# Order of the tokens in a one-layer streaming encoder: five tiles in one pass, or three dense tiles first and tile 3 with the samples after them

## The chip, the cores and the metric

The kernel runs on one core of one Trainium2 chip. The metric is the device time of one execution in microseconds (us). Engines are named as in the profile: PE (TensorE, matmuls), DVE (VectorE), ACT (ScalarE), POOL (GpSimd, which also issues the indirect gathers), SP (SyncE, which issues the other DMAs). Each engine works through its own instructions in their written order and waits on semaphores.

## The reference, cut to what matters

There are 640 tokens of 1024 values: 512 prompt tokens (tiles 0 to 3 of 128) and 128 sample tokens (tile 4: 8 batches of 16, each with 256 cached positions).

```
h  = rmsnorm(x);  z = h @ w_in            # FoX q,k,v,forget | MLA q-latent, kv-latent, rope key
fo = softmax(q k^T / 8 + c[t] - c[s], causal per frame) v        # 8 heads of 64
mo = softmax(q' k'^T / sqrt(96), causal per chunk of 64) v'      # 8 heads, low rank + rope
x  = x + concat(fo, mo) @ w_o
h2 = rmsnorm(x)
# PEER, per token, 8 heads: q = h2 @ w_pq (256 values a head, normalised)
s1, s2 = q[:128] . sub_keys[0], q[128:] . sub_keys[1]            # 128 scores each
top 16 of each half -> 16 x 16 sums -> top 16 -> experts e = 128*i1 + i2, gates g = softmax
x  = x + sum_k gelu(peer_u[e_k] . h2) * g_k * peer_v[e_k]
y  = rmsnorm_final(x)
```

The outputs are y and the new attention state (fk, fv, logf, ckv, krope) of all tokens.

## The kernel before, in words

The kernel is written by hand in one order for each engine, with semaphores between them. Its stages:

1. Projections of all five tiles (L837 to L866), transposes and low-rank queries and keys (L867 to L911).
2. Attention: 40 steps in a written order `plan` (L353). A step is one pair of heads on one query tile (32 of them, query tiles in the order 3, 0, 2, 1) or one batch of samples (8, spread evenly). Three score banks turn round. A step passes through `scores` (PE), `row_max` (DVE), `exponentials` (ACT), `normalise` (DVE), `transpose_probabilities` (PE), `copy_transposed` (ACT), `values` (PE) and `copy_out` (DVE), each a step or two behind the one before. In turn n PE does scores of n, transposes of n-2 and values of n-3 (L996).
3. Output projection and norm of five tiles (`project_out` L1011, `transpose_h2` L1024; DVE L1295 to L1305).
4. PEER choices. For each of 8 heads PE computes queries (L1035 to L1057) and scores (`key_scores`, L1068) for all five tiles, in the order QUERY_ORDER (L72); for each pair of heads DVE takes the top 16 twice (`head_pair`, L1314, with `top16`, L1323) and writes one-hot tiles; POOL turns these into expert numbers (`decode`, L560), but for the last half of the last pair, which DVE does itself (L1393).
5. Gate matrix. The 384 dense tokens (tiles 0 to 2) don't gather their experts: all 16384 experts are computed for them, and a gate matrix of 128 x 128 per token selects. It is formed in 48 turns of 8 tokens (L1413 to L1428): DVE makes one-hots `bsel` and gated one-hots `asel`, ACT scales two of the eight (`scale_two`), PE multiplies them (L1098 to L1110), ACT evicts into `stage` (`evict`, L781), and SP stores `stage` in DRAM every four turns (L465).
6. Dense and sparse loop, 128 blocks (L1132, L1439): PE does dense blocks of 128 experts for tiles 0 to 2, while POOL gathers rows of peer_u and peer_v (L551) and DVE does the dot products and sums for tiles 3 and 4, whose expert numbers are `eidx` (L1407).
7. Final norm and stores of y.

`link` and `step` make DVE wait for its own last instruction. SP's loads stand in one written order (L384 to L495): w_o and the samples' caches during attention, wpq of head h once the queries of head h-2 are done.

Of the kernel before, what the change touches and what calls it, by code (L numbers as in the profile page):

```python
# [6 lines left out]
F32 = mybir.dt.float32  # L29
F32R = mybir.dt.float32r  # L30
# [39 lines left out]
CHUNKS = NTD // CHUNK  # L70

QUERY_ORDER = [("queries", 0), ("scores", 0), ("queries", 1), ("scores", 1)] + [  # L72
    (step, h + n) for h in range(2, PH, 2) for step in ("queries", "scores") for n in range(2)]
PARTS = 4
PART = CHUNK // PARTS
LAST_ORDER = [*range(TD, T), *range(TD)]


def peer_step_kernel(nc, t_in, t_out):

    base, end = 16512, 229344

    class Region:


        def __init__(self, at):
            self.at = at

        def __call__(self, name, shape, dtype=F32):
            size = int(np.prod(shape[1:])) * {F32: 4, F32R: 4, U32: 4, BF16: 2}[dtype]  # L90
            t = nc.alloc_sbuf_tensor_at(name, shape, dtype, offset=self.at)
            self.at += (size + 31) // 32 * 32
            assert self.at <= end, (name, self.at)
            return t

    with ExitStack() as ctx:
# [4 lines left out]
        r = Region(base)  # L101
        ident = r("ident", [P, P])
        ones = r("ones", [P, P])
        small = r("small", [P, 64])
        eps_col = r("eps_col", [P, 8])
        stat = r("stat", [P, 2, 6])
        late_at = r.at

        c_rope = r("c_rope", [P, 2, NT])
        c_rrow = r("c_rrow", [P, 2, T, ROPE // 2])  # L110
        selh = r("selh", [P, FH, P], BF16)
        selb = r("selb", [P, DB, P])
        cb = r("cb", [P, 3 * P + DS], BF16)
        gm = r("gm", [P, KD])
        bfb = r("bfb", [P, T, FH])
        gq = r("gq", [P, QL])
        gkv = r("gkv", [P, KVL])
        fv = r("fv", [P, T, FH * HD])
        zt_at = r.at
        zT = r("zT", [P, T, 4, P])  # L120
        fqT = r("fqT", [P, 4, NT])
        kt_at = r.at
        kT = r("kT", [P, 4, NT])
        ncT = r("ncT", [P, SEQ])
        nc3 = r("nc3", [P, SEQ], BF16)
        nc_mid = r("nc_mid", [P, SEQ], BF16)
        w_uv = r("w_uv", [P, MH * VD])
        wu_at = r.at
        w_uq = r("w_uq", [P, 2, MH, P])
        w_uk = r("w_uk", [P, MH, NOPE])  # L130
        w_ukT = r("w_ukT", [P, MH, P])
        zr_at = r.at
        zr = r("zr", [P, T, RW])
        r2_at = r.at
        krl = r("krl", [P, T, P])
        cqn = r("cqn", [P, T, QL])
        ckvn = r("ckvn", [P, T, KVL])
        fk = r("fk", [P, T, FH * HD])
        a_at = r.at

        z = Region(zr_at)
        qps = z("qps", [P, DB, MH, DS])
        qrs = z("qrs", [P, DB, MH, DS])
        assert z.at <= r2_at

        a1 = Region(a_at)
        hT = a1("hT", [P, KD, NT])
        wv_at = a1.at
        rmsb = a1("rmsb", [P, NT])
        rstdb = a1("rstdb", [P, NT])  # L150
        wr_at = a1.at
        wr = a1("wr", [P, KD, RW])
        wk_at = a1.at
        wk = a1("wk", [P, KD, FH * HD])
        wv = Region(wv_at)("wv", [P, KD, FH * HD])
        assert wv_at + 4 * KD * FH * HD <= wk_at
        sq = Region(a1.at)("sq", [P, KD, NT])
        wk_hi = a1("wk_hi", [P, KD, FH * HD], F32R)
        wq_hi = Region(a1.at - 4 * KD * FH * HD)("wq_hi", [P, KD, FH * HD], F32R)
        wq_at = a1.at  # L160
        wq = a1("wq", [P, KD, FH * HD])
        wr_hi = Region(a1.at)("wr_hi", [P, KD, RW], F32R)
        wv_hi = a1("wv_hi", [P, KD, FH * HD], F32R)
        h_lo = Region(a_at)("h_lo", [P, KD, NT], F32R)
        wr_lo = Region(wr_at)("wr_lo", [P, KD, RW], F32R)
        wk_lo = Region(wk_at)("wk_lo", [P, KD, FH * HD], F32R)
        wv_lo = Region(wv_at)("wv_lo", [P, KD, FH * HD], F32R)
        wq_lo = Region(wq_at)("wq_lo", [P, KD, FH * HD], F32R)
        h_hi2 = [Region(at)(f"h_hi{n}", [P, KD // 2, NT], F32R) for n, at in enumerate((zt_at, kt_at))]
# [5 lines left out]
        a2 = Region(a_at)  # L175
        qmT = a2("qmT", [P, MH, NT])
        kmT = a2("kmT", [P, MH, SEQ])
        vm = a2("vm", [P, TP, MH * VD])
        prob = a2("prob", [P, 6, SEQ])
        probT = a2("probT", [P, 2, 2, SEQ])  # L180
        qbd = a2("qbd", [P, 4, DB, 2, DS])
        oT = a2("oT", [P, 8, NT])
        latT = a2("latT", [P, MH, P])

        s1 = Region(wu_at)
        vs = s1("vs", [P, 2, 2, FH * HD])
        ckTs = s1("ckTs", [P, 2, L])
        krTs = s1("krTs", [P, 2, L])
        assert s1.at <= zr_at
        s2 = Region(r2_at)  # L190
        kTs = s2("kTs", [P, 2, 4, L])
        vn = s2("vn", [P, 2, FH * HD])
        ckr = s2("ckr", [P, 2, 2, KVL])
        ckn = s2("ckn", [P, 2, KVL])
        lfs = s2("lfs", [P, L])
        ncS = s2("ncS", [P, L])
        assert s2.at <= a_at

        l1 = Region(late_at)
        x2 = l1("x2", [P, T, D])  # L200
        h2_at = l1.at
        h2 = l1("h2", [P, T, D])
        gfin = l1("gfin", [P, D])
        gate = l1("gate", [P, T, SEL])
        eidx = l1("eidx", [P, TG * SEL], U32)
        iota = l1("iota", [P, NK])
        gsum = l1("gsum", [P, 2, T * PH])
        ix = l1("ix", [P, PER, GROUP], U32)
        e_at = l1.at
        e1 = l1("e1", [P, T, SEL])  # L210
        e2 = l1("e2", [P, T, SEL])
        gap = l1("gap", [P, T, SEL])
        g_at = l1.at
        gffn = l1("gffn", [P, D])
        h2T = l1("h2T", [P, KD, NT])
        wpq = l1("wpq", [P, 2, KD, 2 * P])
        assert l1.at <= a_at
        l2 = Region(a_at)
        w_o = l2("w_o", [P, 8, D])
        assert l2.at <= a_at + 4 * MH * (NT + SEQ)  # L220
        top_at = end - 2 * 4 * KD * NTD
        hd = Region(top_at)
        hh = hd("hh", [P, KD, NTD], F32R)
        hl = hd("hl", [P, KD, NTD], F32R)

        l3 = Region(a_at)
        pq = l3("pq", [P, 2, 2, NT])
        pq2 = l3("pq2", [P, 2, 2, NT])
        keysT = l3("keysT", [P, 2 * PH, NK])
        scb = l3("scb", [P, 2, T, 2, NK])  # L230
        rt = l3("rt", [P, 2, 8])
        rs = l3("rs", [P, 2, 8])
        sr = l3("sr", [P, 2, T, 2, NK])
        cand_at = l3.at
        cand = l3("cand", [P, 2, T, CAND])
        candr = l3("candr", [P, 2, T, CAND])
        onehot = l3("onehot", [P, 2, T, TK, TK])
        onehot2 = Region(cand_at)("onehot2", [P, 2, T, TK, TK])
        assert TK * TK <= 2 * CAND
        v16 = l3("v16", [P, 2, T, 2, TK])  # L240
        i16 = l3("i16", [P, 2, T, 2, TK], U32)
        i16f = l3("i16f", [P, 2, T, 2, TK])
        cv = l3("cv", [P, 2, T, TK])
        ci = l3("ci", [P, 2, T, TK], U32)
        hi = l3("hi", [P, 2, T, TK], U32)
        lo = l3("lo", [P, 2, T, TK], U32)
        outer = l3("outer", [P, 2, T, TK], U32)
        assert l3.at <= top_at

        k9 = Region(g_at)  # L250
        i1T = k9("i1T", [P, NTD])
        i2T = k9("i2T", [P, NTD])
        gT = k9("gT", [P, NTD])
        bsel = k9("bsel", [P, PARTS, PART, NK])
        asel = k9("asel", [P, PARTS, PART, NK])
        stage = k9("stage", [P, 2, NK, CHUNK])
        assert k9.at <= top_at

        assert h2_at == late_at + 4 * T * D
        rows5 = Region(late_at)("gbuf", [P, 2, T * D])  # L260
        gbuf = rows5[:, :, 0:STEPS * NTD].rearrange("p a (c k t) -> p a c k t", c=CHUNKS, k=STEPS)
        assert TD * D >= STEPS * NTD
        z0 = Region(e_at)
        dots = z0("dots", [P, PER, GROUP])
        gelu = z0("gelu", [P, PER, GROUP])
        wts = z0("wts", [P, PER, GROUP])
        actv = z0("actv", [P, 2, NTD])
        assert z0.at <= g_at
        k10 = Region(g_at)
        vbuf = k10("vbuf", [P, PER, GROUP, D])  # L270
        v_at = k10.at
        vb = k10("vb", [P, PER, D])
        vl = Region(v_at)("vl", [P, PER, D], F32R)
        vh = k10("vh", [P, 2, D], F32R)
        ga = k10("ga", [P, 2, NTD])
        acth = k10("acth", [P, 2, NTD], F32R)
        actl = k10("actl", [P, 2, NTD], F32R)

# [66 lines left out]


        wait_carrier = sem("wait_carrier")

# [1233 lines left out]
```

## Time and profile before

| what | value |
|---|---|
| median of 3 runs | 1989.03 us (1985.73 to 1989.65) |
| the profiled execution's own time | 1997.39 us |
| its span, first to last instruction | 1995.6 us |
| mean granted PE clock | 0.94 of full |
| busy: PE, DVE, ACT, POOL | 1816.5, 1557.1, 768.4, 906.7 us |
| attention; output projection and norm | 208 to 393; 393 to 466 us |
| heads on PE; last pair's rest on DVE | 466 to 686; 686 to 744 us |
| gate matrix; start of the loop | 744 to 888; 888 to 927 us |
| loop, last sums and norm | 927 to 1995.6 us |

Times are read on an axis that begins with the first instruction. The granted clock is a share of full speed: 1.00 is 2.4 GHz and 0.50 is 1.2 GHz; values between are means over a stretch with both.

### The profile page before, as it was taken

How to read it: one execution, taken by the hardware profiler on the slowest of the kernel's cores; microseconds unless marked ns; L12 is line 12 of the kernel's file. 1: busy time of each engine (PE TensorE's matmuls, PEld its weight loads, DVE VectorE, ACT ScalarE, POOL GpSimd, SP SyncE). 2: the span in 40 equal slices, each digit the busy share in tenths (PEclk: the TensorE clock that was granted, in tenths of full speed). 3: DMA queues.
4: the chain of work that ended last, by engine and by line, in shares of the span. 5: the costliest groups of instructions: out<-in, count | busy, mean ns of one | idle time of the engine just before them, and what ended most of it. 6: DMA issues, size and time to landing. Idle time of an engine off the chain costs nothing.

```text
span 1995.6 us, 28371 instructions
## 1 busy us (share of the span) xinstructions
PE 1816.5 (91%) x9103; PEld 1479.4 (74%) x9103; DVE 1557.1 (78%) x3225; ACT 768.4 (39%) x1250; POOL 906.7 (45%) x731
## 2 busy tenths in 40 slices
PE   6999999999899607657999999999999999999998
PEld 4882566645566406655999999999999999999997
DVE  5305343322678889985999999999999999999999
ACT  4321543302111109982434443444344434443443
POOL 0003000000044441004777777777777777777772
PEclk8999887799988759998999999999999999999999
DMA  6110214021110005448999999999999999999994
GB/s 242 43 62 2 84 56 169 33 85 42 43 32 34 1 28 204 185 184 294 392 391 410 404 401 404 400 403 404 398 410 404 395 404 410 403 404 404 410 404 197
DMA packets 159308, 502.60 MB, mean 252 GB/s; under 512 B 17776, under 2 KB 51504, under 8 KB 155536
## 3 DMA queue, kind: packets, MB, share of 16 engines
q0 software_dynamic: 73728, 268.47, 34.2%
q1 hardware_dynamic: 85520, 233.42, 30.5%
q8 instruction: 27, 0.44, 0.1%
q14 instruction: 33, 0.27, 0.0%
HBM read 470.99 MB, written 30.84 MB: 251 GB/s over the span
## 4 chain that ended last, share of the span: by engine, by line
PE 82%; DVE 12%; ACT 2%; issue 2%; DMA 1%; SPq 0%; DVEq 0%; ACTq 0%
PE ps L1125 25%; PE ps L1141 9%; PE ps L1142 9%; PE ps L1143 9%; PE ps L1044 6%; DVE asel L1425 4%; PE ps L1020 3%; DVE bsel L1417 3%; PE ps L863 2%; PE ps L864 2%; PE ps L865 2%; PE ps L963 2%; PE ps L1051 1%; PE ps L988 1%; PE ps L977 1%
## 5 line engine op out<-in xcount | busy, mean ns | idle before, releaser
L552 POOL DMA_INDIRECT vbuf<-in_peer_v,ix x256 | 373.8, 1460 | 221.6 <-DMA gate_matrix<-stage 143.9
L552 POOL DMA_INDIRECT ubuf<-in_peer_u,ix x256 | 371.4, 1451 | 156.4 <-POOL ix L607 109.3
L1141 PE MATMUL ps<-hh,uh 128*128 128x384 f32 x1024 | 346.3, 338 | 10.5 <-DVE ul L1166 10.4
L1142 PE MATMUL ps<-hl,uh 128*128 128x384 f32 x1024 | 345.2, 337 | 0.0
L1143 PE MATMUL ps<-hh,ul 128*128 128x384 f32 x1024 | 344.9, 337 | 0.0
L1449 DVE SCALAR_TENSOR_TENSOR ubuf<-ubuf,h 128x1024 f32<-128x1024 f32 x256 | 302.8, 1221 | 1.1 <-issue 1.1
L1125 PE MATMUL ps<-vh,acth 128*128 128x512 f32 x774 | 240.9, 392 | 0.0
L1125 PE MATMUL ps<-vh,actl 128*128 128x512 f32 x774 | 239.8, 391 | 0.0
L1125 PE MATMUL ps<-vl,acth 128*128 128x512 f32 x774 | 239.7, 391 | 0.0
L1141 PEld LDWEIGHTS ps<-hh,uh 128*128 128x128 f32 x1024 | 193.2, 189 | 17.4 <-DVE ul L1166 12.4
L1142 PEld LDWEIGHTS ps<-hl,uh 128*128 128x128 f32 x1024 | 193.2, 189 | 5.0 <-issue 0.2
L809 ACT ACTIVATE vh<-vb 128x1024 fp32r<-128x1024 f32 x128 | 135.7, 1060 | 154.1 <-PE ps L1125 153.5
L1143 PEld LDWEIGHTS ps<-hh,ul 128*128 128x128 f32 x1024 | 193.2, 189 | 0.0
L1166 DVE TENSOR_TENSOR vl<-vb,vh 128x1024 fp32r<-128x1024 f32 x128 | 156.4, 1222 | 39.3 <-ACT vh L809 28.0
L574 POOL TENSOR_TENSOR onehot<-onehot,i16f 128x2560 f32<-128x2560 f32 x7 | 48.3, 6897 | 301.9 <-DVE onehot L1382 301.9
L1125 PEld LDWEIGHTS ps<-vl,acth 128*128 128x128 f32 x774 | 145.3, 188 | 32.8
L1125 PEld LDWEIGHTS ps<-vh,actl 128*128 128x128 f32 x774 | 145.2, 188 | 31.7
L1469 DVE SCALAR_TENSOR_TENSOR x<-vbuf,wts,x 128x1024 f32 x128 | 163.9, 1280 | 0.0
L1473 DVE SCALAR_TENSOR_TENSOR x<-vbuf,wts,x 128x1024 f32 x128 | 163.8, 1280 | 0.0
L1166 DVE TENSOR_TENSOR ul<-ub,uh 128x1024 fp32r<-128x1024 f32 x129 | 157.4, 1220 | 4.8 <-ACT uh L799 4.8
L1125 PEld LDWEIGHTS ps<-vh,acth 128*128 128x128 f32 x774 | 143.5, 188 | 21.7
L1108 PE MATMUL ps<-asel,bsel 128*128 128x128 f32 x768 | 100.4, 285 | 46.3 <-DVE asel L1425 46.3
(291 smaller groups left out, 2859.5 us busy)
## 6 DMA issues: line engine op xcount, KB each, us to landing
ub<-in_peer_uT SPq DMA_DIRECT2D x129, 512.0 KB
vb<-in_peer_v SPq DMA_DIRECT2D x128, 512.0 KB
gate_matrix<-stage SPq DMA_DIRECT2D x12, 2048.0 KB, 6.3
gbuf<-gate_matrix SPq DMA_DIRECT2D x64, 384.0 KB
wpq<-in_wpq SPq DMA_DIRECT2D x8, 1024.0 KB, 4.9
kTs<-in_past_k SPq DMA_DIRECT2D x8, 512.0 KB, 4.4
vs<-in_past_v SPq DMA_DIRECT2D x8, 512.0 KB, 4.9
w_o<-in_w_o SPq DMA_DIRECT2D x1, 4096.0 KB, 13.6
```

The source lines that it names most:

```text
L552: nc.gpsimd.indirect_dma_start(out=dst[:, slot, e, :], out_offset=None, in_=t_in[table], in_offset=bass.IndirectOffsetOnAxis(ix[:, slot, e ...
L809: A(vh[:, s % 2], vb[:, s], ACT.Copy).then_inc(vh_ready, 1)
L1044: mm(ps[:, c], wpq[:, h % 2, k, c * P:(c + 1) * P], h2T[:, k, 0:SEQ], start=(k == 0), stop=(k == KD - 1))
L1108: last = mm(ps[:, g, k * P:(k + 1) * P], bsel[:, q, tok], asel[:, q, tok], start=True, stop=True)
L1125: ins = mm(ps[:, 2 * d + half], a[:, d * P:(d + 1) * P], v[:, half * 512:(half + 1) * 512], start=False, stop=last_block and n == 2, skip_ ...
L1141: mm(ps[:, 6 + slot, 0:NTD], uh[:, slot, k], hh[:, k], start=(k == 0), stop=False)
L1142: mm(ps[:, 6 + slot, 0:NTD], uh[:, slot, k], hl[:, k], start=False, stop=False)
L1143: last = mm(ps[:, 6 + slot, 0:NTD], ul[:, s, k], hh[:, k], start=False, stop=(k == KD - 1))
L1166: V.tensor_tensor(low, full, high.bitcast(F32), ALU.subtract).then_inc(done, 1)
L1449: ins = V.scalar_tensor_tensor(out=ubuf[:, s, e], in0=ubuf[:, s, e], scalar=1.0, in1=row(h2), op0=ALU.mult, op1=ALU.mult, accum_out=dots[: ...
L1469: V.scalar_tensor_tensor(out=row(x2), in0=vbuf[:, s, 0], scalar=wts[:, s, 0:1], in1=row(x2), op0=ALU.mult, op1=ALU.add).then_inc(half_done, 1)
L1473: V.scalar_tensor_tensor(out=row(x2), in0=vbuf[:, s, 1], scalar=wts[:, s, 1:2], in1=row(x2), op0=ALU.mult, op1=ALU.add).then_inc(acc_done, 1)
```

## The change

Tokens are worked in two groups, X (tiles 0, 1, 2) and Y (tile 3 and the samples). Each group has its own tiles in SBUF, all at addresses written out in a table. The order of the work becomes:

- attention of tiles 0 to 2 (24 steps), output projection, norm and all eight heads' queries and scores of group X; DVE takes the choices of three of the four pairs of heads;
- 16 more attention steps: four MLA steps of tile 3, between which DVE works off the fourth pair's choices in portions of 20 small steps, and then four times a FoX step of tile 3 and two batches of samples. Before the second of these, at step 28, PE transposes group X's gates and expert numbers (`turn_choices`). From step 30 on each step also holds one turn of the gate matrix, 13 turns up to the end of the attention;
- the other 35 turns stand between the stages of group Y (`later()`): its output projection, norm, queries, scores and choices, four turns behind each half of a head.

POOL decodes all of group X's one-hots and all but the last half pair of group Y's. Score banks are three in the first 24 steps and two in the last 16 (each waits for both exponentials of the step before). PE's query and score banks of the heads are double. bsel and asel are two turns deep and not four. ACT issues the stores of the gate matrix. The samples' caches are loaded during the second attention part, w_o twice (4 MB each), the second time after the last attention step, wpq and keysT twice. The loop of 128 blocks is the same but for its tiles' names, and so are the projections at the start (the FoX queries are cut 256 + 384 columns and not 320 + 320). The gathers of peer_u are issued once `eidx` is ready, which now comes after all turns.

```diff
-PARTS = 4
-PART = CHUNK // PARTS
+PART = 8
+TURNS = NTD // PART
+TILES = [(0, 1, 2), (3, 4)]
+PLAN = [(kind, c, i) for kind in ("mla", "fox") for c in range(4) for i in (2, 0, 1)]
+FIRST = len(PLAN)
+PLAN += [("mla", c, 3) for c in range(4)]
+FOX_AGAIN = len(PLAN)
+for c in range(4):
+    PLAN += [("fox", c, 3), ("sample", 2 * c, 0), ("sample", 2 * c + 1, 0)]
+ALL = len(PLAN)
+GATES_FROM = FOX_AGAIN + 2
+IN_SLOTS = ALL + 3 - GATES_FROM
+IN_STEP = 20
...
+        def later():
+            turn = IN_SLOTS
+            behind = {("start", 0): 3, ("out", 3): 1, ("out", 4): 1, ("normed", 3): 1, ("normed", 4): 1, ("queries", 0): 1,
+                      ("scores", 0): 1, ("queries", 1): 1}
+            stages = [("start", 0), ("up", 0), ("out", 3), ("out", 4), ("normed", 3), ("normed", 4),
+                      ("queries", 0), ("scores", 0), ("queries", 1), ("scores", 1)]
+            for h in range(PH):
+                stages.append(("half", h))
+                if h + 2 < PH:
+                    stages += [("queries", h + 2), ("scores", h + 2)]
+                behind[stages[-1]] = 4
+                if h % 2 == 1:
+                    stages.append(("pair", h // 2))
+            for stage_ in stages:
+                yield stage_
+                for _ in range(min(behind.get(stage_, 0), TURNS + 1 - turn)):
+                    yield "gates", turn
+                    turn += 1
...
 @block.sync
+            sp.wait_ge(pv_done, ALL)
+            load_out_weights(1)
+            load_rows(1)
+            load_query_weights(1, 0)
...
 @block.scalar
+            for n_ in range(FIRST, ALL + 3):
+                if n_ == FOX_AGAIN:
+                    gap_exponentials(0)
+                if n_ < ALL:
+                    exponentials(n_)
...
+                k = n_ - GATES_FROM
+                if k >= 0:
+                    scale_two(k)
+                if FIRST + 2 <= n_ < ALL + 2:
+                    copy_transposed(n_ - 2)
+                if k >= 1:
+                    evict(k - 1)
...
 @block.tensor
+            def turn_choices():
+                x = GR[0]
+                pe.wait_ge(topk_done, 1)
+                pe.wait_ge(decoded, PH)
...
+            def sum_gates(k):
+                pe.wait_ge(bsel_ready, k + 1)
...
+                    if k >= 1:
+                        pe.wait_ge(g_copied, 2 * (k - 1) + half + 1)
...
+            for n in range(FIRST, ALL + 3):
+                if n < ALL:
+                    scores(n)
+                if n == FOX_AGAIN:
+                    turn_choices()
+                if FIRST + 2 <= n < ALL + 2:
+                    transpose_probabilities(n - 2)
+                if n > GATES_FROM:
+                    sum_gates(n - GATES_FROM - 1)
+                if n >= FIRST + 3:
+                    values(n - 3)
+            for stage_, x in later():
+                if stage_ == "gates":
+                    sum_gates(x - 1)
...
 @block.vector
+            def make_gates(k):
+                q, first = k % 2, k * PART
+                if k >= 2:
+                    dve.wait_ge(sel_used, 2 * k - 2)
...
+            for pair in range(PH // 2 - 1):
+                for _ in choices(pair):
+                    pass
+            remaining = choices(PH // 2 - 1)
+            for n_ in range(FIRST, ALL + 4):
+                if n_ < FOX_AGAIN:
+                    for _ in range(IN_STEP):
+                        next(remaining, None)
+                if n_ == FOX_AGAIN:
+                    for _ in remaining:
+                        pass
+                    dve.sem_inc(gap_ready, 1)
+                    gate_values(0)
+                if n_ < ALL:
+                    row_max(n_)
+                if FIRST + 1 <= n_ <= ALL:
+                    normalise(n_ - 1)
+                k = n_ - GATES_FROM
+                if 0 <= k < IN_SLOTS:
+                    make_gates(k)
+                if n_ >= FIRST + 4:
+                    copy_out(n_ - 4)
+            for stage_, x in later():
+                if stage_ == "gates":
+                    if x < TURNS:
+                        make_gates(x)
...
+                elif stage_ == "half":
+                    for _ in half_choices(1, x):
+                        pass
+                elif stage_ == "pair":
+                    for _ in pair_choices(1, x):
+                        pass
```

`half_choices` is the old reciprocal and `top16` of one head, `pair_choices` the rest of the old `head_pair`, `make_gates`, `sum_gates` and `evict` one of the old 48 turns on DVE, PE and ACT.

## Rows read from the trace of the kernel before

**Rows 1.** The page's chain of the work that ended last, by line.
```profile
PE ps L1125 25%; PE ps L1141 9%; PE ps L1142 9%; PE ps L1143 9%; PE ps L1044 6%; DVE asel L1425 4%; PE ps L1020 3%; DVE bsel L1417 3%; PE ps L863 2%; PE ps L864 2%; PE ps L865 2%; PE ps L963 2%; PE ps L1051 1%; PE ps L988 1%; PE ps L977 1%
```

**Rows 2.** Windows by stage: length, busy of PE, PEld, DVE, ACT, POOL, granted clock, DMA share, GB/s.
```profile
208.00:393.00 185.00, 179.95 (x1096) 120.08 (x1095) 77.37 (x233) 75.95 (x212) 4.96 (x24) 0.79 0.25 84
...
466.00:686.00 220.00, 199.46 (x840) 131.35 (x840) 154.43 (x832) 35.79 (x51) 63.71 (x31) 0.88 0.10 34
686.00:744.00 58.00, 2.37 (x9) 1.64 (x9) 51.57 (x208) 4.25 (x8) 28.78 (x17) 0.50 0.02 7
744.00:888.00 144.00, 98.76 (x755) 90.05 (x756) 144.00 (x384) 127.39 (x189) 8.83 (x8) 0.98 0.47 190
888.00:927.00 39.00, 16.89 (x70) 11.88 (x68) 8.59 (x12) 9.15 (x11) 8.63 (x8) 0.80 0.80 291
```

**Rows 3.** Chain of waits in the gate matrix: start, length, what.
```profile
746.60 1.13 DVE bsel L1417
...
749.61 1.13 DVE bsel L1417
```

**Rows 4.** PE timeline of the attention: one batch's scores, one batch's values.
```profile
223.47 0.67 PE L947 MATMUL ps<-kTs,qbd 128*32 128x272 f32 x8
...
225.40 0.72 PE L952 MATMUL ps<-krTs,qrs 32*128 32x272 f32 x2
...
233.90 0.53 PE L988 MATMUL ps<-probT,vs 128*128 128x32 f32 x4
...
238.02 0.48 PE L993 MATMUL ps<-probT,ckn 16*128 16x128 f32 x2
```

**Rows 5.** Windows of 2 us behind that batch's values (columns as in rows 2).
```profile
236.00:238.00 2.00, 2.00 (x14) 1.74 (x13) 0.00 (x0) 0.00 (x0) 0.00 (x0) 1.00 0.00 0
246.00:248.00 2.00, 2.00 (x4) 0.81 (x3) 0.69 (x1) 0.21 (x1) 0.00 (x0) 0.50 0.00 0
```

**Rows 6.** Chain of waits in the output projection.
```profile
421.83 13.73 PE ps L1020 x32
435.57 0.87 PE ps L1031 x8
```

**Rows 7.** DVE timeline: first and last instruction of tile 0's norm.
```profile
407.33 1.22 DVE L1297 TENSOR_TENSOR x<-x,ps 128x1024 f32<-128x1024 f32 x1 [14.23 <-PE ps L1020]
...
410.38 1.28 DVE L1304 SCALAR_TENSOR_TENSOR h<-x,small,gffn 128x1024 f32<-128x1024 f32 x1
```

**Rows 8.** PE timeline of one head.
```profile
598.65 13.97 PE L1044 MATMUL ps<-h2T,wpq 128*128 128x512 f32 x32 [2.78 <-ACT pq L750]
...
616.03 2.40 PE L1076 MATMUL ps<-keysT,pq 128*128 128x128 f32 x20
618.27 2.29 PE L1080 MATMUL ps<-ones,pq 128*128 128x1 f32 x20
```

**Rows 9.** DVE timeline: one head's top 16; the rest of a pair.
```profile
496.18 0.19 DVE L1344 RECIPROCAL rs<-rt 128x5 f32<-128x5 f32 x1 [22.50 <-ACT rt L760]
...
508.85 0.28 DVE L1338 FIND_INDEX8 i<-v,sr 128x8 uint32<-128x128 f32 x1
...
702.66 0.56 DVE L1353 TENSOR_TENSOR v<-v,rs 128x160 f32<-128x160 f32 x2
...
723.49 2.82 DVE L1382 TENSOR_TENSOR onehot<-hi,iota 128x2560 f32<-128x2560 uint32 x1
```

**Rows 10.** POOL timeline: first and last instruction of one pair's decoding.
```profile
556.89 7.66 POOL L574 TENSOR_TENSOR onehot<-onehot,i16f 128x2560 f32<-128x2560 f32 x1 [214.21 <-DVE onehot L1382]
...
582.55 0.60 POOL L578 TENSOR_TENSOR e<-onehot 128x80 f32 x2 [0.25 <-POOL onehot L576]
```

**Rows 11.** The page's DMA issues: count, KB, us to landing.
```profile
w_o<-in_w_o SPq DMA_DIRECT2D x1, 4096.0 KB, 13.6
```

**Rows 12.** DVE timeline: a product beside POOL's.
```profile
726.46 7.97 DVE L1393 TENSOR_TENSOR onehot<-onehot,i16f 128x2560 f32<-128x2560 f32 x1
```

**Rows 13.** Chain of waits at the start of the loop.
```profile
913.22 8.83 DMA vb<-in_peer_v
```

More of the change, by code:

```diff
@@ L160, in peer_step_kernel @@
[L160 to L169, printed above, removed]
+        ident = tile("ident", [P, P])
@@ new lines, in peer_step_kernel @@
+        GR = [group(0), group(1)]
+        assert TK * TK <= 2 * CAND
+        gffn = tile("gffn", [P, D])
+        iota = tile("iota", [P, NK])
+        h2X = tile("h2X", [P, 2, D])
+        h2Y = tile("h2Y", [P, TG, D])
+        hh = tile("hh", [P, KD, NTD], F32R)
+        hl = tile("hl", [P, KD, NTD], F32R)
+        eidx = tile("eidx", [P, TG * SEL], U32)
+        gT, i1T, i2T = (tile(n, [P, NTD], at="selT", skip=4 * NTD * k) for k, n in enumerate(("gT", "i1T", "i2T")))
+        bsel = tile("bsel", [P, 2, PART, NK])
@@ new lines, in peer_step_kernel @@
+        asel = tile("asel", [P, 2, PART, NK])
+        stage = [tile(f"stage{k}", [P, NK, CHUNK]) for k in range(2)]
+        x2s, gates = GR[1].x2, GR[1].gate
+        gbuf = tile("gbuf", [P, 2, CHUNKS, STEPS, CHUNK])
+        ubuf = [tile(f"ubuf{s}", [P, GROUP, D]) for s in range(PER)]
+        vbuf = [tile(f"vbuf{s}", [P, GROUP, D]) for s in range(PER)]
+        ub = [tile(f"ub{s}", [P, KD, P]) for s in range(PER)]
+        ul = [tile(f"ul{s}", [P, KD, P], F32R, at=f"ub{s}") for s in range(PER)]
@@ L582, in _ @@
-            with pool.Fori(0, PH // 2 - 1) as pair:
-                decode(pair, ((1, onehot2, e2), (0, onehot, e1)))
-            decode(PH // 2 - 1, ((1, onehot2, e2),))
             pool.wait_ge(eidx_ready, 1)
@@ L726, in _ @@
+            for n_ in range(FIRST + 2):
+                if n_ < FIRST:
                     exponentials(n_)
@@ new lines, in queries @@
+            def queries(g, h):
+                x, out = GR[g], query_bank(g, h)
+                pe.wait_ge(wpq_loaded[h % 2], 16 * (PH // 2 * g + h // 2 + 1))
+                if h == 0:
+                    pe.wait_ge(h2t_copied, 2 * (TILES[g][-1] + 1))
+                    pe.wait_ge(x2_ready, TILES[g][-1] + 1)
+                if h >= 2:
+                    pe.wait_ge(pq_copied, PH * g + h - 1)
+                for c in range(2):
+                    for k in range(KD):
+                        last = mm(out[:, c], x.wpq[h % 2][:, k, c * P:(c + 1) * P], x.h2T[:, k, :],
+                                  start=(k == 0), stop=(k == KD - 1))
+                last.then_inc(pq_done, 1)
@@ L1084, in _ @@
-            for step, h in QUERY_ORDER:
-                if (step, h) != ("queries", 0):
-                    {"queries": queries, "scores": key_scores}[step](h)
-            pe.wait_ge(sc_copied, PH)
-            pe.wait_ge(topk_done, 1)
-            for u, src in enumerate((gate, e1, e2)):
-                if u == 1:
-                    pe.wait_ge(eidx_ready, 1)
-                for t in range(TD):
-                    last = tr(ps[:, u, t * P:(t + 1) * P], src[:, t], ident[:])
-                last.then_inc(selT_done, 1)
@@ new lines, in _ @@
+            for stage_, x in later():
+                if stage_ == "gates":
+                    sum_gates(x - 1)
+                elif stage_ == "up":
+                    pe.wait_ge(o_copied, 8 + ALL - FIRST)
+                    for h in range(MH):
+                        last = mm(ps[64 * (h % 2):64 * (h % 2) + 64, 0, (h // 2) * P:(h // 2 + 1) * P],
+                                  w_uv[:, h * VD:(h + 1) * VD], latT[:, h], start=True, stop=True)
+                    last.then_inc(up_done, 1)
+                elif stage_ == "out":
+                    project_out(x)
+                elif stage_ == "normed":
+                    transpose_h2(x)
+                elif stage_ == "queries":
+                    queries(1, x)
+                elif stage_ == "scores":
+                    key_scores(1, x)
@@ L1430, in _, with choices @@
-            low_part(ul[:, 0], ub[:, 0], uh[:, 0], uh_ready, 1, ul_ready)
-            dve.wait_ge(sel_used, NTD + CHUNK)
-            dve.wait_ge(g_stored, 16 * CHUNKS)
-            for zeros in (acth[:, 1], actl[:, 1], vh[:, 1], vl[:, PER - 1]):
+            for t in TILES[0]:
+                norm(t)
+            dve.wait_ge(keys_loaded, 32)
+            def choices(pair):
+                for s in range(2):
+                    yield from half_choices(0, 2 * pair + s)
+                yield from pair_choices(0, pair)
@@ new lines, in _ @@
+            dve.wait_ge(decoded, 2 * PH - 1)
+            V.scalar_tensor_tensor(out=eidx[:].rearrange("p (t k) -> p t k", t=TG), in0=y.e1[:], scalar=float(NK),
+                                   in1=y.e2[:], op0=ALU.mult, op1=ALU.add).then_inc(eidx_ready, 1)
+            low_part(ul[0][:], ub[0][:], uh[0][:], uh_ready, 1, ul_ready)
+            gate_values(1)
+            for k in range(2):
+                dve.wait_ge(g_stored[k], 8 * CHUNKS)
+            for zeros in (acth[:, 1], actl[:, 1], vh[:, 1], vl[PER - 1][:]):
```

1275 lines of the change are left out of this document (649 added, 626 removed), and 8 rows, old and new, of the table AT.

## The prediction

> **What bounds the kernel now.** I read the chain of waits first: PE holds most of it, and the largest pieces (L1125, L1141 to L1143) are the loop of 128 blocks, which the change leaves as it is; the DVE pieces L1425 and L1417 are the gate matrix [rows 1]. Then the windows by stage, as the question is what can lie beside what [rows 2]. Attention (208 to 393) keeps PE busy 180 of 185 us and DVE 77. The heads (466 to 686) keep PE busy 199 of 220 and DVE 154. Then come 58 us in which PE has 2 us of work, and 144 us of gate matrix with DVE busy all the time. The start of the loop takes 39 us. So DVE holds up 202 us (686 to 888) with PE lightly used, and before that DVE idles 108 us in attention and 66 in the heads. The change wants to lay the one over the other. As the loop is the same, only the path up to 927 us counts; I walk it anew, on the same axis. Up to 211, where attention is in step, both are alike (the FoX queries have the same columns, cut otherwise).
>
> **Attention of tiles 0 to 2.** PE bounds attention. Its work at full clock is about 180 x 0.79 = 143 us [rows 2]. A batch of samples takes 2.6 us for scores (223.5 to 226.1), 4.5 for values (233.9 to 238.4) [rows 4] and 0.7 for transposes, so 7.8, and eight take 62. The other 81 us are 80 units (8 pairs of heads x 10 key tiles over the four query tiles), so 1.0 us a unit. Tiles 0 to 2 have 48 units, so 49 us; I take 61 with the waits of short steps and the last step's way to the output. It ends at 272. Bounds: 54 (PE never waits) and 70 (at the old mean clock).
>
> **Output projection, three tiles.** 3 x 13.73 and twice 0.87 for transposes [rows 6] are 43. The last tile's norm, 4.4 us (407.3 to 411.7) [rows 7], was covered by the first head's queries; that cover is gone, as the queries want all three tiles. 48 in all, to 320.
>
> **Heads of X.** A head's queries were 13.97 us for 512 columns [rows 8]; 384 are 10.5. Scores and squares were 4.7 for 5 tiles, now 2.8. So two heads take PE 26.6 us at full clock. Scores and squares bring the clock down: the stage's mean is 0.88 [rows 2]. Double banks take away PE's waits of 2.8 us. I add 5 a pair for the clock, so 31.6. DVE needs 12.6 us for a head's top 16 in 5 tiles and 23.6 for the rest of a pair [rows 9], so 48.9 a pair; three tiles are 0.6 of that, 29.5. PE and DVE are nearly level. DVE starts after one head's queries, scores and copies, 17 us, and pair 3's first scores come after 8 queries, 7 scores and three low-clock stretches: 84 + 20 + 15 and first copies 5, so 124, to 444. Bounds: 105 (DVE alone) and 140.
>
> **MLA steps of tile 3 with pair 3.** DVE bounds: 29.5, and four times 2.5 for maxima and normalising, so 39.5, to 483.5. PE's 16 us lie under it.
>
> **Transposing the choices.** A new wait. PE may go on only when POOL has decoded pair 3. A decoding of five tiles takes 26.3 us (556.9 to 583.1) [rows 10]; of three 15.8, from about 479. Queued behind it on PE are transposes, values and scores of steps 26 to 29, and DVE waits for these. With the transposes PE resumes at 498.5: 15 us nearly empty. Bounds 10 and 18.
>
> **FoX steps and samples with 13 turns.** PE has 14 us of four FoX steps on tile 3 (16 units, less the first scores), 5 left over from the MLA steps, 62 of samples and 12 turns at 2.05 (98.8 / 48, [rows 2]): 105 us at full clock. DVE has 71 us, so PE bounds. Now the clock. Before, it stood at 1.00 during a batch's values and at 0.50 right behind them, for 10.6 us there (238.6 to 249.2) [rows 5]. Such a stretch stands behind each of the eight batches, 9.8 us on the mean. Batches now come two in three steps. One cycle (FoX, sample, sample, three turns, 25.4 us at full clock) has two low stretches that each cost 4.9 us: 35 us. In all 141.5, to 640. Bounds: 110 (the clock holds) and 184 (it never comes back).
>
> **Group Y with the other 35 turns.** DVE's work: 35 x 3.01 = 105 (746.60 to 749.61) [rows 3], two norms 9, the hl subtraction and a copy 4, eight top 16 of two tiles 8 x 5.2 = 42, four pair rests 4 x 9.8 = 39, the last product, sums and eidx 5.5: 205. What it waits for: w_o starts only when the last attention step is done and takes 13.6 [rows 11], then the projection 13.7, with three turns to fill the time: 19 idle. The second tile's projection against one turn and a norm: 9. Queries and scores of the first two heads (7.0 and 1.9 each on PE) against the turns, two deep: 10, when turn 24 wants turn 22 summed and PE is in head 2's queries. Small ones: 5. Sum 248, with 4 for gaps 252.5, to 892.5. PE has 17 us a head against DVE's 22, ACT 13, so neither takes over. Bounds: 236 and 275.
>
> **POOL beside the turns.** DVE's product of 2560 elements beside POOL's took 7.97 us [rows 12], the one-hot compare of the same size 2.82 [rows 9]; POOL's own product took 7.66 [rows 10]. These slow each other. In group Y a decoding (10.5 us) starts behind a pair, half beside the top 16 and half beside the turns, three times. I charge 5 us in all, to 897.5; bounds 0 and 31 (all of it, 3 x 10.5). The Trainium skill, "SBUF — State Buffer", section "Who interferes with whom", says that a DVE instruction with two SBUF inputs and a GpSimd instruction that reads SBUF shut each other out for a whole instruction. bsel and onehot are of that kind; the 7.97 us agree, and by the rule the time is 15 to 31 us above what it is without contention, rival 3 below.
>
> **Start of the loop.** It was 39 us from the last turn. PE's fold of x2 and the last stores are now done earlier; the numbers of the gathers come later. After eidx: 6 us for DVE (low part, gates, zeros), 4 for SP's issues, 8.8 for vb to land [rows 13], 5 for ACT's and DVE's parts: 24. The gathers of peer_u, formerly done long before, run beside it. PE's second block starts at 922 and not 927. Bounds 20 and 35, the high one if 4 MB more of gathers delay vb.
>
> **Sum.** 211 + 61 + 48 + 124 + 39.5 + 15 + 141.5 + 252.5 + 5 + 24 = 921.5, 5 us before 927. The span becomes 1990.5 and the profiled execution 1992.4 against 1997.4. That one was 8.4 above the median, which stands for the whole: 1989 - 5 = 1984 us. That 144 us of turns are moved and 5 won has three reasons, which the reader can check in the sum: 35 of 48 turns stay on DVE's own path; the 15 us at step 28, the 28 us in front of group Y's norms and the 12 at the heads' start are new; and samples that come close together keep PE's clock low.
>
> **Rivals.**
> 1. The clock holds in the steps with samples. For: in the gate matrix PE was busy 99 of 144 us and had a mean clock of 0.98 [rows 2], and turns now stand between. Against: [rows 5]. Then 110 and not 141.5: 1953 us.
> 2. Slower: the clock doesn't come back between samples. Place: the twelve steps from 28 on. Price: a sample step at 0.50 is 4.8 + 1.5 + 4.1 + 7.3 = 17.7, the FoX step 10.4, a cycle 45.7, the stage 184: 42 us, 2026. It decides from the point where two low stretches meet: a sample's scores, transposes and turn, 5.4 us of work, must take longer than the low stretch lasts, 10.8 against 9.8 on the mean, so it is near. For: some low stretches lasted 14 us. Against: FoX steps with a dense turn stand between.
> 3. POOL and DVE shut each other out wherever they meet: 15 to 26 more, 2004 us. For: [rows 12]. Against: half of the decoding lies beside top 16, whose 12.7 us a head were the same with POOL busy or not.
> 4. It doesn't do what it says: DVE was as needed before as after, no stretch is really covered, 1989 us.
>
> **How the numbers follow.** What a measurement can tell from no change is 0.2%, 4 us. Forecast (within 15 us of 1984) 0.45; rival 1 0.27; rival 2 0.14; rival 3 0.11; rival 4 0.03. The forecast's own range, 1969 to 1999, gives 0.24 faster, 0.11 same, 0.10 slower; rival 1 gives 0.27 faster (less 0.01 for errors elsewhere); rivals 2 and 3 0.24 slower; the rest same. So 0.50 faster, 0.15 same, 0.35 slower. The range reaches to 1943, rival 1 with the low bounds of the heads, and to 2018, which leaves out the end of rival 2.
>
> **What would show it.** Right: the last turn some 20 us before eidx at about 895; the first 24 attention steps over by 272; an empty PE before step 28's transposes; clock 0.7 to 0.8 in the samples; DVE idle near 28 us while w_o and the two projections run; the loop's blocks as long as before. Wrong: a granted clock near 1.00 or near 0.50 between 500 and 640; bsel instructions well above 1.2 us; DVE waiting for sel_used in every head; or a loop whose blocks take longer than before.

## The result, and the profile after

The change made the kernel slower: 2003.6 us median of 4 executions (2001.58 to 2004.25) against 1989.2 us (1985.73 to 1989.65) for the kernel before, ratio 1.0075, 95% interval 1.0057 to 1.0092. Run once more with other executions of both, the ratio was 1.0095 (1.0062 to 1.0128). The forecast was 1984 us, 5 us faster, within 1969 to 1999. The profiled execution took 2003.8 us, span 2002.0.

The way up to the loop came out as forecast: PE's second dense block, from which on the loop runs evenly, started at 923.3 (forecast 922, in the first trace of before 926.9). The forecast missed in two things that it took over from before unchanged: the length of the loop's blocks, and how far a profiled execution lies above the median. First the windows of the kernel after, by its stages (columns as in [rows 2]):

```profile
211.00:268.00 57.00, 53.66 (x428) 35.96 (x428) 37.53 (x126) 37.03 (x119) 0.00 (x0) 0.94 0.26 107
268.00:317.00 49.00, 44.28 (x120) 20.80 (x121) 11.96 (x16) 4.38 (x10) 0.00 (x0) 1.00 0.07 23
317.00:433.00 116.00, 108.05 (x452) 71.36 (x452) 87.08 (x483) 21.45 (x40) 33.54 (x25) 0.99 0.25 85
433.00:466.00 33.00, 14.55 (x44) 7.23 (x44) 32.10 (x169) 6.54 (x14) 15.39 (x18) 0.64 0.14 42
466.00:483.00 17.00, 3.26 (x8) 0.89 (x8) 15.37 (x16) 4.22 (x10) 15.98 (x11) 0.63 0.00 0
483.00:613.00 130.00, 128.86 (x796) 100.06 (x797) 66.11 (x193) 57.37 (x119) 4.88 (x20) 0.79 0.32 111
613.00:887.00 274.00, 190.56 (x1067) 157.25 (x1066) 215.46 (x746) 115.46 (x185) 43.10 (x43) 0.87 0.32 126
887.00:923.00 36.00, 10.46 (x42) 9.35 (x42) 9.18 (x14) 4.50 (x4) 18.74 (x20) 0.64 0.94 346
```

The bare 144 us of gate matrix are gone, but PE is idle no less than before: from 211 to 887 it is busy 543.2 us, in the same stretch of the kernel before 550.8. In place of the gate matrix stand 274 us of group Y in which DVE is busy for 215, and 36 us at the loop's start with the DMA engines busy 0.94 of the time and PE 10 us.

Now the loop. The rows are the chain of waits: start and length of the 18 matmuls that each block does with peer_v (below: the values part; the 24 with peer_u are its dense part). The first rows are the kernel before, traced again (control below), the second the kernel after.

```profile
1003.38 4.12 PE ps L1125 x18
...
1011.66 4.12 PE ps L1125 x18
...
1019.95 4.12 PE ps L1125 x18
```

```profile
1005.17 4.18 PE ps L1225 x18
...
1013.56 4.18 PE ps L1225 x18
...
1021.93 4.16 PE ps L1225 x18
```

A block is 8.285 us before and 8.38 us after, although its instructions are the same, PE never waits in these stretches and the granted clock is 1.00 in both. Over the loop the kernel after lost 10.1 us: 1078.7 against 1068.7 from the second dense block to the end (2002.0 - 923.3, 1995.6 - 926.9).

At the loop's start PE waits for the first block of peer_v (PE timeline; chain of waits):

```profile
892.97 0.66 PE L1241 MATMUL ps<-hh,uh 128*128 128x384 f32 x1 [18.91 <-DVEq L1599]
...
923.27 0.69 PE L1241 MATMUL ps<-hh,uh 128*128 128x384 f32 x1 [19.84 <-DVE ul L1265]
```

```profile
898.14 20.23 DMA vb<-in_peer_v
```

That load took 8.83 us in [rows 13]. In group Y, DVE's waits (engine, line, releaser: us in all, times, longest):

```profile
DVE x2Y L1398 <- PE ps L1093: 26.6, 2, 18.6
DVE bsel L1509 <- PE ps L1162: 25.3, 9, 10.7
DVE oTY L1385 <- PE ps L1079: 8.2, 1, 8.2
```

The last of these ends at 612.5, as group Y begins, and belongs to the samples. Where POOL decodes, the chain of waits, and POOL's own instruction at that time:

```profile
751.28 3.40 DVE bsel L1509
754.67 1.39 DVE asel L1511
756.07 1.72 DVE asel L1516 x4
```

```profile
751.25 2.34 POOL L587 TENSOR_TENSOR onehotY<-onehotY,i16fY 128x1024 f32<-128x1024 f32 x1
```

bsel took 1.13 in [rows 3], with POOL idle; beside POOL it took 3.40, three times (751, 805, 858).

### The profile page after: what moved, and what is told of

Same layout as the page of the kernel before. It is cut to its first block, busy times and chain, and to the rows that moved or that the text cites. A ratio compares the mean times of both kernels' runs of the same rounds, so it can differ in the third digit from the quotient of the medians.

```text
span 2002.0 us, 28007 instructions
## 1 busy us (share of the span) xinstructions
PE 1811.4 (90%) x9103; PEld 1499.5 (75%) x9103; DVE 1584.2 (79%) x3299; ACT 772.1 (39%) x1277; POOL 952.5 (48%) x779
## 4 chain that ended last, share of the span: by engine, by line
PE 80%; DVE 13%; DMA 2%; ACT 2%; POOL 1%; issue 1%; SPq 0%; DVEq 0%; ACTq 0%; POOLq 0%
PE ps L1225 26%; PE ps L1241 9%; PE ps L1242 9%; PE ps L1243 9%; PE ps L1118 4%; PE ps L1093 4%; PE ps L1162 3%; PE ps L943 2%; PE ps L945 2%; PE ps L944 2%; PE ps L1074 1%; DVE bsel L1509 1%; PE ps L1050 1%; DVE asel L1516 1%; DMA vb<-in_peer_v 1%
## 5 line engine op out<-in xcount | busy, mean ns | idle before, releaser
L627 POOL DMA_INDIRECT ubuf<-in_peer_u,ix x256 | 382.6, 1494 | 156.2 <-POOL ix L652 109.1
L627 POOL DMA_INDIRECT vbuf<-in_peer_v,ix x256 | 395.1, 1543 | 78.0 <-issue 78.0
L1611 DVE SCALAR_TENSOR_TENSOR ubuf<-ubuf,h2Y 128x1024 f32<-128x1024 f32 x256 | 302.8, 1221 | 5.3 <-DMA ubuf<-in_peer_u,ix 5.3
L1162 PE MATMUL ps<-asel,bsel 128*128 128x128 f32 x768 | 114.0, 311 | 58.9 <-DVE asel L1516 41.3
L1635 DVE SCALAR_TENSOR_TENSOR x2Y<-vbuf,wts,x2Y 128x1024 f32 x128 | 163.8, 1280 | 0.0
L1631 DVE SCALAR_TENSOR_TENSOR x2Y<-vbuf,wts,x2Y 128x1024 f32 x128 | 163.8, 1280 | 0.0
L1162 PEld LDWEIGHTS ps<-asel,bsel 128*128 128x128 f32 x768 | 107.8, 223 | 64.8 <-issue 64.4
```

Of the source, the lines that this page charges most:

```text
L627: nc.gpsimd.indirect_dma_start(out=dst[slot][:, e, :], out_offset=None, in_=t_in[table], in_offset=bass.IndirectOffsetOnAxis(ix[:, slot, e ...
L1162: last = mm(ps[:, 6 + half, j * P:(j + 1) * P], bsel[:, k % 2, tok], asel[:, k % 2, tok], start=True, stop=True)
L1611: ins = V.scalar_tensor_tensor(out=ubuf[s][:, e], in0=ubuf[s][:, e], scalar=1.0, in1=row(h2Y), op0=ALU.mult, op1=ALU.mult, accum_out=dots[ ...
L1631: V.scalar_tensor_tensor(out=row(x2s), in0=vbuf[s][:, 0], scalar=wts[:, s, 0:1], in1=row(x2s), op0=ALU.mult, op1=ALU.add).then_inc(half_do ...
L1635: V.scalar_tensor_tensor(out=row(x2s), in0=vbuf[s][:, 1], scalar=wts[:, s, 1:2], in1=row(x2s), op0=ALU.mult, op1=ALU.add).then_inc(acc_don ...
```

## The experiments

**The kernel before, traced again.** No edit.

> The kernel before, unchanged, profiled once more. In the first trace of it a block of the loop took 8.29 us, and its profiled execution was 8.4 us above the median of the others; in the kernel after a block took 8.35 to 8.40 us. Theory A (the block's length belongs to the kernel): 8.29 us here again. Theory B (it belongs to the chip or the execution): another length, 8.35 or more being possible. If the 8.4 us above the median were a property of the execution and not of profiling, the span is now near 1987 instead of 1995.6, and the windows show which stage got shorter.

Span 1991.0, second dense block 922.7, 8.285 us a block: the block's length belongs to the kernel. Beside it, 22 executions of before gave 1980.5 to 1999.5 us, clock 0.948 for the fastest and 0.938 and 0.939 for the two slowest. A third trace:

> The kernel before, unchanged, a third trace of it. Over 22 executions it took 1980.5 to 1999.5 us and the granted clock of each was the lower the longer it took (0.948 to 0.938). Theory: the difference lies in the stretches ahead of the gate matrix, where the clock falls behind samples and scores: the mark of the first expert numbers (eidx, 740.9 in the first trace, 736.7 in the second) moves with the span, and the loop's blocks are 8.29 us again. Rival: the difference lies in the loop.

Span 1987.3, eidx at 730.8 (740.9 in the first trace, 736.7 in the second), second dense block at 917.6. Blocks as before. Its attention window:

```profile
208.00:393.00 185.00, 179.75 (x1114) 119.15 (x1114) 77.48 (x233) 76.18 (x212) 4.97 (x24) 0.83 0.28 96
```

Mean clock 0.83 where [rows 2] have 0.79, and the output projection began at 385.7 and not 393.3. So 7.6 us of the 8.3 by which the spans differ (1995.6 and 1987.3) are attention with its samples. This execution (1989.2 us) lies at the median; the trace on which the prediction rests had its surplus in just the stage that the change rebuilds.

**Addresses in the loop.** First hh and hl alone:

```diff
-        top_at = end - 2 * 4 * KD * NTD
+        top_at = end - 2 * 4 * KD * NTD - 224
```

> The kernel before with hh and hl alone placed 224 bytes lower in SBUF (their addresses become multiples of 256, as in the kernel after). Theory A1 (the low address bits of what PE reads set the pace of its matmuls in the loop): the dense matmuls of 384 columns go from 173.3 ns to 175 or more apart, some 24 x 2 = 50 ns a block, 6 us in all; the values' matmuls of 512 columns stay at 227 to 236 ns. Theory A2 (only the weights' addresses, or none): 8.29 us a block and the same time within 2 us.

Dense matmuls went from 173.3 to 176.6 ns, as A1 wants; but the first nine of the values' matmuls, whose own addresses are untouched, went from 232 to 227 ns, where A1 had them stay. A block took 8.32 us; ratio to before 1.0013 (0.9991 to 1.0036). Next all of them, in the kernel before:

```diff
+        def low_bits(region, want):
+            region.at += (want - region.at) % 256
-        ub = k10("ub", [P, PER, KD, P])
+        ub = slots(k10, "ub", [P, KD, P], F32, (64, 64, 128, 192))
...
+        low_bits(k10, 64)
         acth = k10("acth", [P, 2, NTD], F32R)
+        low_bits(k10, 192)
         actl = k10("actl", [P, 2, NTD], F32R)
```

> The kernel before with every tile that PE reads in the loop (hh, hl, uh, ub, vh, vb, acth, actl) moved by less than 256 bytes each, so that its address modulo 256 is that of the kernel after; order and work unchanged. Theory A1 (low address bits): a block takes 8.35 to 8.40 us and not 8.29, the whole 8 to 13 us more than before. Theory C (the longer block comes from the order of gathers and loads at the loop's start, or from the other engines' state in it): 8.29 us, no difference.

```profile
1008.04 4.18 PE ps L1147 x18
...
1016.41 4.15 PE ps L1147 x18
...
1024.77 4.18 PE ps L1147 x18
```

Blocks in the four buffers of ub and vb took 8.39, 8.35, 8.38 and 8.39 us in turn, matmul by matmul the pattern of the kernel after. The whole: ratio 1.0057 (1.0025 to 1.0088). The kernel before, with nothing changed but addresses modulo 256, has lost most of what the change lost. Is it TensorE alone?

```diff
+            for w in R:
+                for m in R:
+                    for _ in range(2):
+                        dense(w, m)
```

> TensorE alone: no other engine works and nothing is computed (all tiles are zeros). The loop's dense pattern (24 matmuls of 384 columns) and its values pattern (18 of 512) run for all 64 pairs of addresses modulo 256 of what is loaded as weights and what is streamed, in steps of 32 bytes, and then whole blocks at the addresses of some kernels. Theory A1 (TensorE's own reads collide by low address bits): the pace depends on the pair; weights 64 with streamed 224 gives 173.3 ns a dense matmul, 64 with 0 gives 176.4, the best pair N + 32 cycles throughout (173.3 and 226.7 ns), so a block of 8.24 us. Theory A2 (the addresses only set how TensorE meets the other engines' and the DMAs' accesses): one pace for all pairs.

Yes. Nanoseconds from one start to the next, by the distance (streamed address less weights' address) modulo 256, worked out from the starts in the trace:

```
distance           0      32      64      96     128     160     192     224
384 columns    173.3   173.3   173.3   176.7   176.1   173.3   174.6   173.3
512 columns    226.7   233.4   228.7   233.4   233.4   234.4   233.3   233.2
```

Of the 64 pairs for 384 columns two are off this table (176.7 at distances 160 and 32), of those for 512 only by 1 or 2 ns. The table holds for a run of like matmuls. In whole blocks the two parts also shift each other: the addresses of before gave 8.29 us, where the table adds up to 8.24 and 8.24 was expected, those of b_moving 8.32 (distance 192 in the dense part: 174.6 ns in the table, 176.7 in the block), others 8.29 to 8.37. Why they do is open. A2 is out: with the other engines idle the addresses alone change the pace. The Trainium skill, "SBUF — State Buffer", section "Who interferes with whom", gives TensorE two independent read ports, for streamed operand and weights, and knows one contention only, that of the pair shared by VectorE and GpSimd; by it all pairs of addresses would be alike. The measurement decides: they are not. Then the cure, in the kernel after:

```diff
-    "uh0": 80128, "uh1": 84224, "acth": 90944, "ub0": 94016, "vh": 165248, "actl": 197056,
+    "uh0": 80224, "uh1": 84320, "acth": 90976, "ub0": 94048, "vh": 165472, "actl": 197216,
...
```

> The kernel after with the tiles that TensorE reads in the loop moved by 32 to 224 bytes each, so that every weight tile (uh, ub, acth, actl) and vh, vb lie at 96 modulo 256 and hh, hl at 0: the distances of the kernel before (160 in the dense part, 0 in the values). Order of the work unchanged. Theory (TensorE's own reads collide by address distance modulo 256): a block takes 8.29 us again and not 8.38, the whole 10 to 13 us less than after: 1991 to 1994. Rival (in this kernel the blocks are also held by DVE or the gathers, whose order differs): less than 5 us.

```profile
1006.52 4.12 PE ps L1225 x18
...
1014.80 4.12 PE ps L1225 x18
...
1023.09 4.14 PE ps L1225 x18
```

8.29 us a block, as expected. The whole took 1995.7 us (1991.4 to 2001.6), above the 1991 to 1994 expected; ratio to before 1.0024 (1.0002 to 1.0046) where after has 1.0075. That is 10 us less than after by the ratios and 8 by the medians, and in the traces the loop from the third dense block on takes 1060.3 and not 1068.2. A little of the rival holds: some 126 blocks should have given 11 us, but three times in this trace a load of vb came late (ACT waited 6 us for it), and the blocks behind it took 1.0 to 1.3 us more in all. The trace of control has one such place, that of after has none. (hh and hl stay at 0; vb, ub and their neighbours move likewise. The order was not quite unchanged: besides the addresses, eidx went to another place and ACT's `gap_exponentials(1)` ahead of its first uh. The way from eidx to the second dense block is 37.1 us, in after 36.8.)

**The first loads.** SP's wait for eidx moved behind the first vb, the counters that let gbuf and ub start set before it, gfin loaded behind the loop.

```diff
-            sp.wait_ge(eidx_ready, 1)
-            ld(gfin[:], t_in["gfin"]).then_inc(x2_loaded, 16)
...
                         ld(vb[s][:], ...).then_inc(vb_loaded[s], 16)
+                        if step == 0:
+                            sp.wait_ge(eidx_ready, 1)
```

> The kernel after with the first loads of the loop (gate matrix rows, second block of peer_uT, first block of peer_v) no longer behind the expert numbers: SP issues them once the gate matrix is stored, some 10 us ahead of eidx. Theory: vb's 20.2 us (898.1 to 918.4) were 6 MB of gathers and loads in front of it; with it landed at about 890, PE's second dense block starts at 905 to 910 and not 923, so 13 to 18 us less than after (1986 to 1991). Rival: the loop is held back by peer_u's and peer_v's gathers, which still start at eidx; then the stall comes back in the first blocks and less than 8 us are won.

```profile
906.30 0.45 PE L1242 MATMUL ps<-hh,uh 128*128 128x384 f32 x1 [0.87 <-DVE ul L1266]
```

1987.7 us (1986.9 to 1994.0), ratio 0.9993 (0.9979 to 1.0008): 16 us less than after by the medians. The first vb is there by 891.7, and the second dense block starts at 906.3. Part of the rival holds too: the third starts at 922.0, 15.7 behind the second, and DVE waits 7.3 us for the first rows of peer_u and 7.6 for those of peer_v. Still the third comes 33.3 us after eidx, in after 47.3 (933.8 less 886.5). The traced execution is the slowest of the ten (1994.0); from eidx to the end it takes 12 us less than after's. The edit moves all these loads at once, so it doesn't tell the gathers in front of vb from SP's own loads.

**Turns and POOL.**

```diff
-                behind[stages[-1]] = 4
+                behind[stages[-1]] = 8 * (h % 2)
```

> The kernel after with the turns of the gate matrix in group Y eight behind every second half of a pair, and none behind the first, so that POOL decodes a pair of group Y beside the top 16 of the next two halves and not beside turns. Theory (POOL and DVE exclude each other): the three bsel of 3.40 us fall back to 1.22 and the asel behind them too, 12 us less of DVE work. Against it, PE's queries of two heads (18 us) now stand in one piece beside 10.4 us of top 16, and DVE's turns wait for them, 2 to 6 us a pair. Sum 0 to 8 us less than after: 1996 to 2004. Rival (PE's order bounds): slower than after.

```profile
620.00:878.00 258.00, 189.99 (x1070) 155.57 (x1069) 203.50 (x747) 115.20 (x185) 40.40 (x42) 0.91 0.35 136
```

1987.4 us (1983.9 to 1995.1), ratio 0.9986 (0.9967 to 1.0006): 16 us less than after by the medians. From the last sample's values to eidx it takes 257.5 us (620.5 to 878.0) where after took 274.1. (That the samples end 8 us later than in after is not the edit's doing: with the same edit they end at 612.8 in a_all_three.) DVE's busy time falls by 12 (215.5 to 203.5), no bsel takes over 1.5, and bsel waits 16.6 us for PE and not 25.3. I had expected that wait to grow; it shrank, so the gain was twice the most that I had expected.

**What the 13 hidden turns buy.**

```diff
-GATES_FROM = FOX_AGAIN + 2
+GATES_FROM = ALL + 2
...
-                behind[stages[-1]] = 4
+                behind[stages[-1]] = 5
```

> The kernel after with none of the turns between the attention steps: one behind them, and five instead of four behind each half of a head in group Y. Theory (as the prediction has it): the steps with samples lose 12 turns of PE, 25 us at full clock and some more at the old mean of 0.79, 25 to 32 us; group Y gains 12 turns of 3.01 us on DVE, 36 us. So 4 to 11 us slower than after: the 13 hidden turns bought little. Rival (the clock falls further without the turns between samples, mean under 0.7): 20 to 35 us slower. Rival (turns cost the samples stage their full wait time through the score banks): faster than after by 5 or more.

```profile
483.00:604.00 121.00, 117.92 (x603) 85.17 (x604) 30.63 (x98) 27.90 (x71) 6.93 (x23) 0.66 0.23 69
604.00:914.00 310.00, 216.05 (x1260) 181.09 (x1259) 251.84 (x843) 145.91 (x233) 43.11 (x42) 0.89 0.33 131
```

2031.5 us, ratio 1.0195 (1.0164 to 1.0226): 28 us slower than after by the medians, 24 by the ratios, so the rival with the clock holds. Without turns between them the samples keep the clock at 0.66 and not 0.79, and their stage (to the last sample's values, 485.7 to 603.7, where after has 483.4 to 612.4) gets only 11 us shorter with 12 turns fewer; group Y gets 36 us longer. A turn between samples costs under 1 us of time and saves 3 in group Y.

**After again, and all three edits.**

> The kernel after, unchanged, once more beside before, so that the edits are compared over several jobs. Its four executions lay between 2001.6 and 2004.3, those of before between 1980 and 1999 with the mean granted clock of each (0.948 for the fastest, 0.938 for the slowest). Theory: before's profiled execution was a slow one by its clock, 7 us above its median, and after's is near its own, so after's median is 2000 to 2004 again and the ratio 1.005 to 1.009. Rival: after varies as much, and its first four were slow ones: median 1995 or less.

2004.2 us (2003.6 to 2007.2), ratio 1.0095, a little more than expected: after lies near its own profile, and the rival is out.

> The kernel after with all three edits together: the first loads of the loop ahead of the expert numbers, the turns in eights, the aligned tiles. They lie in three separate stretches (group Y, the loop's start, the loop's blocks), so the theory adds them: 16 + 16 + 11 = 43 us less than after, 1960, and 30 us less than before (ratio 0.985). Rival (they share a bound: a shorter way to the loop makes the gathers late in the first blocks): 1970 to 1978.

1965.3 us (1961.9 to 1967.0), ratio to before 0.9858 (0.9829 to 0.9886): 1.4% faster than before, 25 us by the medians of the executions run beside it, and 38 us faster than after. That lies between the theory and the rival. By the stages of the traces, group Y is 17.6 us shorter than in after, the way from eidx to the third dense block 9.9 and the rest of the loop 11.1. Some 4 us are lost together, and the third dense block shows where: it comes 37.4 us after eidx and not 33.3 as in a_early_loads, the second starting at 888.1 and the third at 906.7. The chain of waits between them:

```profile
884.26 14.69 DMA vbuf<-in_peer_v,ix
```

PE's values wait for DVE, and DVE for these gathered rows of peer_v, which are issued once eidx is there.

## Why the prediction was wrong

| step | forecast, us | measured, us |
|---|---|---|
| attention of tiles 0 to 2 | 61, to 272 | to 268.4 |
| output projection | 48 | 48.6, to 317.0 |
| heads up to pair 3 | 124 | 115.8, to 432.8 |
| MLA steps and pair 3 | 39.5 | 35.1, to 467.9 |
| stall at step 28 | 15 | 15.5, to 483.4 |
| FoX steps and samples | 141.5 | 129.0, to 612.4 |
| group Y, POOL's share in it | 257.5 | 274.1, to 886.5 |
| start of the loop | 24 | 36.8, to 923.3 |
| loop to the end | 1068.7, unchanged | 1078.7 |
| profiled execution above the median | 8.4 | 0.2 |

**The step that failed in direction** is the one from the path to the whole. "As the loop is the same, only the path up to 927 us counts" was true of the loop's instructions and false of its addresses: every tile has a new place in the table, and that was given no price. It cost 10.1 us. Longer blocks stood among the signs of being wrong, but neither in the sum nor among the rivals. And "8.4 above the median, which stands for the whole" carried a constant over that is none: the surplus lay in attention, 7.6 of 8.3 us, and I worked attention out anew. Measured against an execution near the median (second dense block at 917.6), the forecast 922 was already 4 us slower than before, not 5 faster; the kernel after is 5.7 us behind it there and 14.7 at the end (spans 2002.0 and 1987.3). 10.1 + 8.2 + 1.3 (923.3 for the 922 of the forecast) are the 19.6 us between 1984 and 2003.6.

**Heads and MLA steps** were 12.6 us too long. Of the heads' 124 us, 15 were charged for a low clock; the window 317 to 433 has 0.99, and the rest took 7 us more than forecast. The 4.4 us of the MLA steps I did not follow up. Why the scores no longer bring the clock down I did not test; new against [rows 2], where it was 0.88, are three tiles for five and double banks.

**Step 28** was right in size and place. PE's timeline there:

```profile
483.44 0.88 PE L1147 MATMUL ps<-ident,gateX 128*128 128x128 f32 x3 [10.07 <-POOL e1X L592]
```

The transposes of the gates wait 10.07 us for POOL's last numbers, and PE had stood 5.13 just before.

**Samples** were 12 us too long. The mean clock 0.79 lies in the 0.7 to 0.8 foretold, so rivals 1 and 2 are both out. Two low stretches a cycle came as foretold, but shorter: the first two last 6.8 us each (514.7 to 521.5 and 525.0 to 531.8) where 9.8 was taken, so each costs 3.4 us and not 4.9. By the mean clock the low stretches cost 27 us of the 130, where the sum had 36.5 (141.5 less 105); that is 9 of the 12 us. Inside the two, and between them:

```profile
515.00:521.00 6.00, 6.00 (x23) 4.59 (x23) 4.13 (x13) 2.34 (x7) 0.74 (x3) 0.50 0.68 225
522.00:524.00 2.00, 2.00 (x17) 1.84 (x15) 0.00 (x0) 1.24 (x2) 0.00 (x0) 1.00 0.00 1
526.00:531.00 5.00, 5.00 (x17) 2.42 (x17) 0.74 (x2) 0.00 (x0) 0.00 (x0) 0.50 0.41 137
```

a_turns_late shows that the turns held the clock up.

**Group Y** was 17 us too short, by two terms of 7 and 15 us; the others together were 5 too long. POOL beside the turns was 12 us, not 5, within the bound of 31: rival 3 in kind, though not in full. The rule of the Trainium skill ("SBUF — State Buffer", "Who interferes with whom") that was weighed there agrees with it: 3.40 us for bsel are its own 1.13 and POOL's 2.34. The least that was worked out by it, 15 us, was not reached. That the whole came out at rival 3's 2004 us is chance: POOL has 7 us of the 20 between 1984 and 2004. a_turns_in_eights, which parts POOL and the turns, gives 12 us of DVE time back. And turns waited 25 us for PE, nine times, where I allowed 10 for the first heads only: five of these waits are over 2 us, the longest 10.7 (at 706), and by PE's written order 7 us of queries stand in front of the turns of most heads. Long bsel and waits for PE were both named as signs of being wrong. The 26.6 us that DVE waits for the projections were foretold as 28.

**Start of the loop**: vb landed in 20.2 us, not 8.8, and up to 4 MB of peer_u's gathers and 2.5 MB of SP's own loads (gfin, gbuf, ub) were issued in front of it. The bound of 35 for this stage named that case and was passed by 2 us; a_early_loads shows that the place behind eidx was the cause, not which of the two held vb up.

That the path up to the loop was forecast within 2 us is luck: errors of -3.6, +0.6, -8.2, -4.4, +0.5, -12.5, +16.6 and +12.8 us cancelled.

## What to carry to other kernels

When a change moves tiles, compare the addresses modulo 256 of what TensorE streams and of its weights before calling any stage unchanged; in this loop, bound by matmuls, that was worth 10 us of 2000. The distance alone didn't give the pace of a whole block here, so a new layout has to be measured. Take the baseline of each stage from an execution near the median, since a surplus over it lies in one stage and doesn't carry over to a rebuilt one. Turns laid between the samples paid, since they kept the clock up: 12 of them cost 11 us and saved 36. Turns that met POOL or stood behind long pieces of PE's order cost more than forecast.

## What the runs showed of the hardware

TensorE's pace depends on the distance modulo 256 bytes between streamed operand and weights, with all other engines idle: 173.3 to 176.7 ns for 384 columns, 226.7 to 234.4 ns for 512, both with fp32r operands and in steps of 32 bytes. What ran before has a part in it (distance 192: 174.6 ns among its like, 176.7 in a block). That these are collisions of its two reads is inferred; the dependence is measured. Executions of one unchanged program ranged over 19 us (1980.5 to 1999.5) with granted clocks from 0.948 to 0.938; where two traces of it differ by 8.3 us, 7.6 lie in the attention with samples.
